# A second output projection turned to tokens on the partitions, its two norms as row sums, and a joined order of the recurrence stage

## The reference, cut to what matters

```
h = modulate(rms_norm(x, pre_norm_mix), sh1, sc1)
z = h @ w_in            # g_rnn, x_rnn, q, three k/v pairs, gate logits
a = exp(log_a);  log_a = -8 * sigmoid(..) * softplus(-lambda)
u = sqrt(-expm1(2 * log_a)) * (sigmoid(..) * conv(x_rnn))
rnn = gelu(g_rnn) * scan(a, u)             # h_t = a_t * h_(t-1) + u_t
att = nsa_attention(q, ...)                # compressed, selected, window branch
y = concat(rms_norm(rnn), rms_norm(att)) @ w_out
x = x + (1 + g1) * rms_norm(y, post_norm_mix)
h = modulate(rms_norm(x, pre_norm_mlp), sh2, sc2)
x = x + (1 + g2) * rms_norm(square(relu(h @ w_ff1)) @ w_ff2, post_norm_mlp)
```

## Time and profile before

| | us |
|---|---|
| median of three runs | 1856.67 (1856.37 to 1857.27) |
| the profiled execution | 1863.7 |
| span of the profile in it | 1861.6 |
| TensorE busy (97% of the span) | 1805.1 |
| VectorE, ScalarE, GpSimd busy | 1031.1, 778.7, 885.8 |
| granted clock, mean | 0.983 |

### The profile page before, as it was taken

The page is one execution under the profiler, slowest core; times in us unless marked ns, Lnnn a source line. Parts: engine busy times, 40 slices in busy tenths (PEclk is TensorE's granted clock), DMA queues, the critical chain, the costliest instruction groups (busy, mean ns, idle before and its releaser), DMA issues. The chain is left out here.

```text
span 1861.6 us, 25409 instructions
## 1 busy us (share of the span) xinstructions
PE 1805.1 (97%) x8617; PEld 1449.5 (78%) x8617; DVE 1031.1 (55%) x1798; ACT 778.7 (42%) x1244; POOL 885.8 (48%) x1158
## 2 busy tenths in 40 slices
PE   7999999999999999999999999999999899999997
PEld 6777888888888877788888888867656778888886
DVE  4787756666657347676666655654675542222234
ACT  4434543333335334443333333485666343232233
POOL 5443445565556543265556555357102335555551
PEclk9999999999999999999999999999999789999999
DMA  7221224443422221123444423122101212222311
GB/s 248 91 91 46 80 71 155 146 158 130 140 91 91 91 91 70 63 72 139 156 146 158 140 95 115 60 102 93 45 1 46 91 38 98 90 90 90 105 75 46
DMA packets 102022, 183.50 MB, mean 99 GB/s; under 512 B 6794, under 2 KB 66748, under 8 KB 99900
## 3 DMA queue, kind: packets, MB, share of 16 engines
q1 hardware_dynamic: 101772, 181.80, 27.8%
q10 hardware_dynamic: 176, 0.73, 0.1%
HBM read 180.42 MB, written 2.10 MB: 98 GB/s over the span
## 5 line engine op out<-in xcount | busy, mean ns | idle before, releaser
L849 POOL TENSOR_TENSOR w_lo<-raw,w_hi 128x256 fp32r<-128x256 f32 (+1 forms) x1148 | 882.9, 804 | 943.4 <-ACT w_hi L886 943.3
L2065 PE MATMUL ps<-n_hi,w_hi 128*128 128x512 f32 x1464 | 584.8, 399 | 6.8 <-DVE n_lo L1418 2.6
L2067 PE MATMUL ps<-n_hi,w_lo 128*128 128x512 f32 x1464 | 572.6, 391 | 0.0
L2066 PE MATMUL ps<-n_lo,w_hi 128*128 128x512 f32 x1464 | 572.4, 391 | 0.0
L886 ACT ACTIVATE w_hi<-raw 128x1024 fp32r<-128x1024 f32 (+2 forms) x331 | 307.4, 936 | 299.2 <-PE ps L2067 177.8
L2065 PEld LDWEIGHTS ps<-n_hi,w_hi 128*128 128x128 f32 x1464 | 276.0, 189 | 69.3 <-issue 10.2
L2067 PEld LDWEIGHTS ps<-n_hi,w_lo 128*128 128x128 f32 x1464 | 275.5, 188 | 59.2
L2066 PEld LDWEIGHTS ps<-n_lo,w_hi 128*128 128x128 f32 x1464 | 275.7, 188 | 58.8 <-issue 3.3
L2065 PE MATMUL ps<-x_hi,w_hi 128*128 128x512 f32 x640 | 254.5, 398 | 0.1
L2067 PE MATMUL ps<-x_hi,w_lo 128*128 128x512 f32 x640 | 249.4, 390 | 0.0
L2066 PE MATMUL ps<-x_lo,w_hi 128*128 128x512 f32 x640 | 249.3, 390 | 0.0
(11 more groups left out here) (288 smaller groups left out, 1877.3 us busy)
## 6 DMA issues: line engine op xcount, KB each, us to landing
raw<-in_w_up SPq DMA_DIRECT2D x44, 1024.0 KB, 6.8
raw<-in_w_ff SPq DMA_DIRECT2D x32, 1024.0 KB, 6.0
raw<-in_w_in SPq DMA_DIRECT2D x26, 1024.0 KB, 7.1
zb<-in_ada_w SPq DMA_DIRECT2D x16, 1536.0 KB, 7.9
raw<-in_w_down SPq DMA_DIRECT2D x44, 512.0 KB, 4.0
raw<-in_w_out SPq DMA_DIRECT2D x12, 1024.0 KB, 5.9
raw<-in_w_in SPq DMA_DIRECT2D x4, 512.0 KB, 9.9
za<-in_x SPq DMA_DIRECT2D x4, 512.0 KB, 7.9
```

The costliest lines, as they stand in the source:

```text
L849: last = pool.tensor_tensor(parts[0][:, c], parts[1][:, c], parts[2][:, c], ALU.subtract)
L2065: pe.matmul(out, l_hi, r_hi, start=start, stop=False)
L2066: pe.matmul(out, l_hi, r_lo, start=False, stop=False)
L2067: return pe.matmul(out, l_lo, r_hi, start=False, stop=stop)
```

## The change

1. **Joined order of the recurrence stage.** The quarters of `kvs`, `cmp` 0, `kw`, `cmp` 1 and `g_rnn` are mixed (`MIXED`), so that a `cmp` quarter stands between two others, on all engines. All gate products come early. Each feature tile has its own buffers; the sigmoids of all tiles, then all Tanh and Exp, then all roots are made together. The factor is now sqrt(tanh(z/2)) multiplied by (1 + a), without a reciprocal. Squares, sums and root of the recurrent branch's norm move ahead of the units, and the first three products of query 1 too.
2. **Projection with tokens on the partitions.** `out2r` and `out2` are multiplied as 4 token tiles x 2 halves of 512 output features, with the activations as stationary operand and the weights moving (`row_products`, weights cut as kind "H").
3. **Norms by row sums.** The sum over features is now along a row: ScalarE's Square has an accumulator (`y_square`, `h_squares`). GpSimd multiplies y by a row of gains (`row_gains`), VectorE scales by the token's factor and adds into `out_rows` (`new_rows`). `h` is transposed to rows between the projection's products (`h_rows`).
4. **Second factor in the turn back.** The new rows are brought back to features on the partitions by a float32 product with a diagonal of the second factor (`scaled_columns`), which transposes and scales at once. ScalarE reads the banks, adds shift and gain, and makes the high part and the full value; VectorE makes the low part. `streamed_first` are 12 matmuls whose result is not used.

```diff
+MIXED = [("kvs", 0), ("kvs", 1), ("kvs", 2), ("cmp0", 0), ("kvs", 3), ("cmp0", 1), ("kw", 0), ("cmp0", 2),
+         ("kw", 1), ("cmp0", 3), ("kw", 2), ("cmp1", 0), ("g_rnn", 0), ("cmp1", 1), ("g_rnn", 1), ("cmp1", 2),
+         ("g_rnn", 2), ("cmp1", 3), ("g_rnn", 3)]
...
-    add(("out2r",), "D4", 4)
-    add(("out2",), "D4", 4)
+    add(("out2r",), "H", 4)
+    add(("out2",), "H", 4)
...
+    if kind == "H":
+        v = raw[:, :].rearrange("p (k c) -> p k c", k=4)
+        return v[:, 2 * (q % 2):2 * (q % 2) + 2, (q // 2) * S:(q // 2 + 1) * S]
...
+            def row_gains():
+                for half in range(2):
+                    emptied(pool, ("pg1_row", half))
+                for t, half in GAINED:
+                    emptied(pool, ("out2", half, t))
+                    pool.tensor_tensor(y_gain[t][half], y_token[t][half], pg1_row[half], ALU.mult).then_inc(y_gained, 1)
...
+                    if g == STR["ff1", 0].g0:
+                        row_gains()
...
             def decay(t):
                 if t == 0:
                     act.wait_ge(sp_ready, 1)
-                else:
-                    act.wait_ge(rnn_ready, t)
                 emptied(act, ("ra", t))
-                act.activation(rn[2], rn[0], ACT.Exp, scale=spt[:, 20 + t:21 + t])
-                act.activation(rn[3], rn[0], ACT.Tanh, scale=spt[:, 24 + t:25 + t]).then_inc(decay_ready, 1)
+                act.activation(roots[t], decays[t], ACT.Tanh, scale=spt[:, 24 + t:25 + t])
+                act.activation(decays[t], decays[t], ACT.Exp, scale=spt[:, 20 + t:21 + t]).then_inc(decay_ready, 1)
             def decay_root(t):
-                act.wait_ge(ratio_ready, t + 1)
-                act.activation(rn[4], rn[4], ACT.Sqrt, bias=zero1, scale=2.0).then_inc(rootm_ready, 1)
+                act.wait_ge(decay_ready, t + 1)
+                act.activation(roots[t], roots[t], ACT.Sqrt, bias=zero1).then_inc(rootm_ready, 1)
...
+            def gated(t):
+                act.wait_ge(rnn_ready, t + 1)
+                act.activation(inputs[t], filled(act, ("g_rnn", t))[:, :], ACT.Gelu_apprx_tanh)\
+                    .then_inc(freed(("g_rnn", t)), 1)
...
+            squares(("rnn",), lambda f: gr[:, f, :], lambda f: (gr_ready, f + 1))
+            block_turned(1)
+            root(("rnn",), HALF)
+            act.activation(more[:, 143:144], zero1, ACT.Exp)
             queries(0)
+            block_out(1)
...
+            def y_square(t, half):
+                emptied(act, ("out2", half, t))
+                act.activation(squared[NT * half + t], y_token[t][half], ACT.Square, scale=D ** -0.5,
+                               accum_out=ysum[:, half, t:t + 1]).then_inc(y_squared, 1)
+            def y_rows_root(t):
+                act.wait_ge(y_eps, 1)
+                act.wait_ge(y_squared, NT + t + 1)
+                act.activation(rt[:, t:t + 1], ysum[:, 1, t:t + 1], ACT.Sqrt, bias=ms[:, t:t + 1]).then_inc(y_root, 1)
+            def h_squares(t):
+                for half in range(2):
+                    act.wait_ge(rows_set, 2 * t + half + 1)
+                    act.activation(squared[2 * t + half], out_rows[:, t, half * S:half * S + S], ACT.Square, scale=D ** -0.5,
+                                   accum_out=hsum[:, half, t:t + 1]).then_inc(h_squared, 1)
+                act.wait_ge(h_eps, t + 1)
+                act.wait_ge(h_squared, 2 * t + 2)
+                act.activation(rt[:, NT + t:NT + t + 1], hsum[:, 1, t:t + 1], ACT.Sqrt, bias=ms[:, NT + t:NT + t + 1])\
+                    .then_inc(h_root, 1)
...
             for f in range(DT):
-                ring_square(("mlp",), f, h[:, f, :], (h_set, DT + f + 1))
-                if f >= 2:
-                    to_rows(out_rows, ("hT", f - 2), f - 2)
-            root(("mlp",), D)
-            for f in range(DT - 2, DT):
-                to_rows(out_rows, ("hT", f), f)
-            split_tiles(("mlp",), DT, 0, lambda f: mod[:, 24 + f:25 + f])
+                k = SPL["mlp",] + f
+                shift, gain = mod[:, 24 + f:25 + f], gs2[:, f:f + 1]
+                b = filled(act, ("hN", f))
+                act.activation(n_hi[:, f, :], b[:, :], ACT.Identity, bias=shift, scale=gain).then_inc(hi_ready, 1)
+                act.wait_ge(lo_ready, k - 2)
+                act.activation(tb[:, k % 3, :], b[:, :], ACT.Identity, bias=shift, scale=gain).then_inc(val_ready, 1)
...
+                link(dve.scalar_tensor_tensor(roots[t], decays[t], 1.0, roots[t], ALU.add, ALU.mult))
+                link(dve.tensor_tensor(inputs[t], inputs[t], roots[t], ALU.mult))
+                dve.tensor_tensor_scan(gr[:, t, :], decays[t], inputs[t], 0.0, ALU.mult, ALU.add).then_inc(rnn_ready, 1)
...
+            def y_add(t, half):
+                emptied(dve, ("out2r", half * NT + t))
+                dve.tensor_tensor(y_token[t][half], y_rnn[half * NT + t], filled(dve, ("out2", half, t))[:, :], ALU.add)\
+                    .then_inc(freed(("out2", half, t)), 1)
+            def new_rows(t):
+                dve.wait_ge(y_root, t + 1)
+                link(dve.reciprocal(rstd[:, t:t + 1], rt[:, t:t + 1]))
+                for half in range(2):
+                    if t == 0:
+                        for f in range(HT * half, HT * half + HT):
+                            emptied(dve, ("hT", f))
+                    dve.wait_ge(y_gained, GAINED.index((t, half)) + 1)
+                    part = out_rows[:, t, half * S:half * S + S]
+                    dve.scalar_tensor_tensor(part, y_gain[t][half], rstd[:, t:t + 1], part, ALU.mult, ALU.add)\
+                        .then_inc(rows_set, 1)
+                dve.wait_ge(h_squared, 2 * t + 1)
+                dve.tensor_scalar(ms[:, NT + t:NT + t + 1], hsum[:, 0, t:t + 1], EPS, None, ALU.add).then_inc(h_eps, 1)
+            def row_factor(t):
+                dve.wait_ge(h_root, t + 1)
+                link(dve.reciprocal(rstd[:, NT + t:NT + t + 1], rt[:, NT + t:NT + t + 1]))
+                dve.tensor_scalar(diag[:, t, :], ident, rstd[:, NT + t:NT + t + 1], None, ALU.mult)\
+                    .then_inc(diag_ready, 1)
+            y_add(1, 1)
+            new_rows(0)
+            y_add(2, 1)
+            new_rows(1)
+            row_factor(0)
+            y_add(3, 1)
+            new_rows(2)
+            row_factor(1)
+            new_rows(3)
+            row_factor(2)
+            row_factor(3)
+            for f in range(DT):
+                k = SPL["mlp",] + f
+                dve.wait_ge(val_ready, k + 1)
+                split_lo(k, tb[:, k % 3, :], n_hi.bitcast(F32)[:, f, :], n_lo[:, f, :])
...
+            block_products(0, 0, 1)
+            narrow(("vsel",), STR["kvs",].at[3], P)
+            block_products(0, 1, 2)
+            features([("kw",)], STR["kw",].at[0])
+            block_products(0, 2, 3)
             narrow_rows("vsel")
-            narrow(("vwin",), STR["kw",].g0 + 1, P)
+            narrow(("vwin",), STR["kw",].at[1], P)
+            block_products(0, 3, 4)
+            narrow(("gates",), STR["kw",].at[2], 24)
+            block_products(1, 0, 1)
+            narrow_rows("vwin")
+            features([("g_rnn", 0)], STR["g_rnn",].at[0])
             block_turn(0)
-            recurrence_gates(3)
-            narrow(("gates",), STR["kw",].g0 + 2, 24)
-            narrow_rows("vwin")
-            block_products(1)
+            block_products(1, 1, 2)
+            narrow_rows("gates")
+            features([("g_rnn", 1)], STR["g_rnn",].at[1])
             block_results(0)
-            features([("g_rnn", 0)], STR["g_rnn",].g0)
-            narrow_rows("gates")
-            features([("g_rnn", 1)], STR["g_rnn",].g0 + 1)
+            block_products(1, 2, 3)
+            features([("g_rnn", 2)], STR["g_rnn",].at[2])
+            block_products(1, 3, 4)
+            features([("g_rnn", 3)], STR["g_rnn",].at[3])
...
+            query_products(0, 0, 3)
+            block_turn(1)
+            query_products(0, 3, 4)
+            norm_sums(("rnn",))
+            query_products(0, 7, 1)
+            block_results(1)
...
+            def row_products(name, key, half, t, first, count):
                 if first == 0:
+                    bank(key)
+                out = ps[BK[key][0]]
                 for k in range(first, first + count):
+                    wh, wl = quarter(STR[name,].g0 + 2 * half + k // 2)
+                    c = k % 2 * S
+                    last = product(out[:, :], n_hi[:, k, t * P:(t + 1) * P], n_lo[:, k, t * P:(t + 1) * P],
+                                   wh[:, c:c + S], wl[:, c:c + S], k == 0, k == HT - 1)
                 if first + count == HT:
+                    if t == NT - 1:
+                        last.then_inc(quarter_done, 2)
+                    else:
+                        last.then_inc(full[BK[key][0]], 1)
...
+            pe.wait_ge(h_set, DT)
+            for half in range(2):
+                gain_row(half)
+            h_rows(0)
             for k in range(HT):
```

(73 more changed lines are left out.)

344 lines of the change are left out of this document (182 added, 162 removed).

## The result

The changed kernel takes 1848.18 us (median of 7 runs, 1845.74 to 1852.11); beside it the kernel before took 1858.76 (7 runs, 1856.37 to 1863.60). The ratio is 0.9938, 95% interval 0.9923 to 0.9952: 11.5 us faster, between 8.9 and 14.3. I had forecast 28 us and a range of 1820 to 1841, so the direction was right and the size was not.

What follows compares the result with a forecast made beforehand. TensorE, busy 97% of the span, was taken as the bound, so only its waits and slow clock could be gained: 12.2 (recurrence end) + 15.9 (tail) = 28.1 us, 1856.67 to 1829; own range 1821 to 1837, wider range 1820 to 1841.

Steps and rivals of the forecast that it cites:

- the recurrence end: Recurrence stage and first units: mixed order removes waits and slow clock, 12.2 us gained, bounds 6 and 16.6.
- the tail: Second projection to first feed-forward tiles: first `ff1` product at 1480.5 against 1497.28; 15.9 us gained, bounds 9 and 19.
- Sum of new waits 3.2: Recurrence stage: waits of 1.3 at `g_rnn` 0, 0.9 at `q2`, 1.0 at the units' start; bounds 0 and 8.
- Old waits and slow clock: Recurrence stage before: 8.7 us of idle TensorE and 5.4 us lost to the clock, both expected to go.
- At `g_rnn` 0 I had 1.3: Recurrence stage: `cmp` 1 and `g_rnn` land about 1250.5, splits of 1.05 and 2.8 follow, TensorE ready at 1253.3.
- For `q2` I had 0.9: End of recurrence stage: `q2` let go at 1272, landed 1279, split 1283, wanted 1282; 0.9 us of wait.
- Behind each `ensure` that waits stand ScalarE's own copies: ScalarE's list in the recurrence stage: reason for adding 1.0 us of wait for the start of the units.
- only change place: Recurrence stage: products of query 1 and the 8 sum matmuls move there, with no gain or cost counted.
- Rival C: Recurrence stage: with ScalarE times 3 us late, landings of `cmp` 1, `g_rnn`, `q2` show, 10.5 us, 1839; chance 0.08.
- The early units: Units 0 to 4: recurrent norm's squares, root and two table loads leave; 1.3 us gained, bounds 0 and 2.5.
- a term that I had at 0.8: Norms after the projection: VectorE's waits for ScalarE's squares, 0.8 us ahead of the last diagonal at 1476.5.
- Rival B: Between projection and feed-forward: TensorE's clock falls to 1.2 GHz between diagonals, costing 5 us, 1834; chance 0.14.

Runs made afterwards that it cites:

- the two halves: Each against the kernel before: only second projection, norms and second factor changed, 1849.56 us; only the joined recurrence order with its norm ahead of the units, 1860.22 us.
- the experiment: The changed kernel without GpSimd's eight multiplications by the gain row, VectorE's update reading the sum itself: 1847.65 us, ratio 0.9934 to the kernel before.
- the tail alone: The kernel before with only the second projection, norms and second factor of the change, its recurrence stage kept: 1849.56 us, ratio 0.9941.

## Why the forecast was wrong

By the times of the two halves, the recurrence end brought nothing (between 2.4 us lost and 1.5 gained) where I had 12.2, and the tail 11.0 where I had 15.9. So the recurrence end owns the larger part of the miss.

**The step that failed** is "Sum of new waits 3.2; their bounds are 0 and 8. Net: 8.7 + 5.4 - 3.2 = 10.9". The new waits were 3.8 + 3.3 + 1.3 = 8.4, outside my own bounds, and the clock that I had at 1.00 was 0.96 over 91.7 us, 3.7 lost: 12.1 us where I put 3.2. Old waits and slow clock went as I said, and came back in full. To compare times, those of the changed kernel are set back by 2.1 us below, since its stage starts at 1214.7 and not at 1212.6. Three things were mis-sized or missing in it:

- At `g_rnn` 0 I had 1.3, and it was 3.8. I let the buffers go at 1238 and 1240; it was 1238.9 and 1240.5, and the two stripes had landed at 1252.2, not 1250.5. But TensorE was ready as much later, at 1255.0 and not at 1253.3, so the late landing added nothing to my 1.3. The 2.5 us more are the low part of `g_rnn` 0: I took 2.8 us, and GpSimd needed 5.32, with VectorE at work on the recurrence. A quarter beside VectorE stood in the trace of the kernel before, at 4.43 us, and I had priced by the shorter ones:

```profile
1242.67 4.43 POOL L849 TENSOR_TENSOR w_lo<-raw,w_hi 128x256 fp32r<-128x256 f32 x4 [1.27 <-ACT w_hi L886]
```

- For `q2` I had 0.9, at `q2` 0, with the buffer let go at 1272 and the stripe landed at 1279. It was 1273.9 and 1282.8, and the wait, 3.3, showed earlier, at `g_rnn` 3, through ScalarE's list and bank 1. "Behind each `ensure` that waits stand ScalarE's own copies" was the right thought, priced at 1.0 and in the wrong place.
- The chain to the norm's sums I had moved at no cost ("only change place"). In the old order the norm was made in units 0 to 4; in the new one the wait for it was 1.3, and 2.2 to 2.8 as soon as the wait before it went.

Rival C named one mechanism (landings, 10.5 us) and its price was about right for this stage, but I gave it 0.08, and its condition, times on ScalarE late by 3 us, was not met: the buffers went 0.5 to 1.9 us late. Its size was right partly by luck, since 2.5 us of the waits came from the low part at `g_rnn` 0. That the placing of the pieces and not the idea was at fault was shown by the kernels with other banks, another ScalarE list and another order: 81.4 us, within 1 us of what I had forecast ("first unit near 1295" from 1212.6 is 82.4).

One bound was also added up wrongly. "Its own range is 1821 to 1837" has 1837 where both lower bounds, 6 and 9, give 1856.67 - 15 = 1841.7.

**The early units**, 1.3 forecast: nothing, 1.0 more of idle. Their waits of 1.3 and 1.5 stand in every profile with the new order: one for VectorE's weighting in the first unit (L2061), one for ScalarE's copy of a query (L1235). In the kernel before, the waits for the same two are 1.0 and 0.3. That the norm's squares and root had caused them I had only assumed.

**The tail**, 15.9 forecast, 13.4 in the profile, 11.0 by the times. How much of the difference between these two is the clock stays open: profiles of other kernels with this tail have it at 0.79 and 0.81 there, this one at 1.00. Projection: 25.2 forecast from first to last product, 25.3 measured, with 28 transposes at full clock. From there to `ff1` 12.6 forecast, 15.9 measured; then 13.0 forecast and 12.1 measured for the first two tiles. The 3.3 us lie ahead of the last diagonal, which came 12.1 us after the last product and not 8.6. VectorE's operations from 1461 to 1477.7, beside the updates shown above:

```profile
L2103 DVE TENSOR_SCALAR ss<-const,rstd 128x128 f32<-128x128 f32 x4 | 1.9, 487 | 0.1
L2088 DVE RECIPROCAL rstd<-rt 128x1 f32<-128x1 f32 x4 | 0.6, 156 | 1.2 <-ACT rt L1404 1.2
L2102 DVE RECIPROCAL rstd<-rt 128x1 f32<-128x1 f32 x4 | 0.6, 153 | 0.5 <-ACT rt L1413 0.5
L2098 DVE TENSOR_SCALAR ms<-small 128x1 f32<-128x1 f32 x4 | 0.6, 148 | 1.0 <-ACT sq L1409 0.9
```

The largest part is a term that I had at 0.8: VectorE waited for ScalarE's squares and roots for 1.2 + 0.5 + 0.9 = 2.6 us. The eight updates took 9.0 and not 8.0; my 1.0 each had already paid part of the ports, so the 1.7 us of the experiment are not this difference. The addition that starts the chain ended 4.3 us before the last product, and not 4.8; the rest, about 0.3, are the small operations, of which a diagonal took 0.49 on the mean where 0.29 is the price of one alone. No run takes these parts singly. Rival B did not occur in the profile of the changed kernel (clock 1.00), and did in that of the tail alone, with the streamed matmuls that I had set against it.

**What the profile was to show**: table loads in the stage 7, right; the large reciprocals gone, right; 12 transposes ahead of the first `out2` product, right; idle under 4 us, clock 1.00 and a first unit near 1295, wrong; 12 to 14 us to `ff1`, wrong by 2.

## What to carry to other kernels

When a change joins two streams of weights, write down for each stripe when its buffer is let go, when it lands with the bandwidth shared with its neighbour, and what lies behind the waiting split in that engine's list: here freed engines were worth nothing while a landing was bare. Price each split by rows in which the neighbouring engine is at work as it will be (5.32 us here, not 2.8). With the piece of the longest matmuls behind the later landing, the wait at `g_rnn` 0 was gone. A wait taken out is worth only the distance to the next one: here 3.3 us at `g_rnn` 3 brought nothing that the times can tell until the norm's chain moved as well. A gain forecast as the removal of all waits in a stage should be checked with the new order's own schedule, and its bounds set by that.

## What the runs showed of the hardware

- The pair of ports of VectorE and GpSimd behaved as a lock: 1.80 us for an operation of 0.75, behind a multiplication of 1.29 that was not stretched.
- GpSimd's pieces of 128 x 256 took 1.33 us each beside VectorE's two-input operations and scans, and 0.70 once VectorE rested.
- With two stripes under way together, the 1 MB transfers of the second took 9.0 and 10.3 us to land, against medians of 6.1 to 6.5 in the kernel before; 0.5 MB pieces took 4.0 to 4.7 (medians).
- TensorE's clock was not a fixed answer to a wait: after idle stretches of 2.7 us it stayed at 2.4 GHz in the changed kernel's tail and fell to 1.2 in the same place with the same eight streamed matmuls in another; behind a wait of 2.2 us in the recurrence stage of the kernel with ScalarE's list changed it was at 1.2, too; behind the waits of 3.8 and 3.3 us in the changed kernel it fell both times (0.50 from 1260.8 to 1264.1 and from 1288.1 to 1291.4).
